# Second attention: weight products in halves over two steps, weight splits at places of their own, the last square summed alone

## The reference, cut to what matters

```python
qg = rms_norm_2(x, norm_g) @ w_in              # 1024 -> 2048: queries and gates
q, gate = qg[..., :DIFF_WIDTH], qg[..., DIFF_WIDTH:]
scores = einsum("qd,kd->qk", q_hi, k_hi) / 8 - slope[h] * |qpos - kpos|     # for h in 8 heads, i in 2
probs = softmax(where(allowed, scores, -inf))
weights = probs[:, :, 0] - lam * probs[:, :, 1]
out = einsum("qk,ke->qe", weights, v)          # per block of 128 queries and head
out = rms_norm_2(out, sub_g) * (1.0 - lambda_init)
x = x + (out * silu(gate)) @ w_out
return rms_norm_2(x, final_norm_g)             # the last norm of the whole model
```

## Time and profile before

| what | value |
|---|---|
| time, median of 3 runs | 2152.75 us (2152.07 to 2153.59) |
| the profiled execution | 2152.05 us, of it 2150.2 us from first to last instruction |
| PE busy | 2006.3 us (93%) |
| DVE busy | 1397.0 us (65%) |
| ACT busy | 856.6 us (40%) |
| mean granted TensorE clock | 0.974 of full |
| the loop of the second attention, 1918.8 to 2111.7 us | 192.90 us, PE busy 173.69, DVE 139.11, ACT 108.30 |

### The profile page before, as it was taken

How to read it: one execution, slowest core, us unless ns; L and a number is a source line. 1 busy time by engine, 2 the same in 40 slices (tenths; PEclk the granted TensorE clock), 3 DMA queues, 4 the chain that set the end, 5 groups by cost and what they waited for, 6 DMA issues and landing times.

```text
span 2150.2 us, 24817 instructions
## 1 busy us (share of the span) xinstructions
PE 2006.3 (93%) x9332; PEld 1574.0 (73%) x9332; DVE 1397.0 (65%) x2060; ACT 856.6 (40%) x1332; POOL 264.8 (12%) x241
## 2 busy tenths in 40 slices
PE   6789999999999999999999999989999989999887
PEld 4567878888887766778888886767777767876555
DVE  7895467536645458657636646877877786437875
ACT  4454333222233348633222234434343434236653
POOL 5130100000010000010000000333323232000002
PEclk9897999999999999999999999999999999999998
DMA  5364323233232220023232222212222213321002
GB/s 195 108 136 119 107 79 108 81 106 98 80 107 98 89 79 1 20 80 107 82 115 91 84 91 81 68 54 64 70 68 69 75 54 98 98 89 39 30 25 74
DMA packets 79479, 178.33 MB, mean 83 GB/s; under 512 B 17664, under 2 KB 31104, under 8 KB 79360
## 3 DMA queue, kind: packets, MB, share of 16 engines
q1 hardware_dynamic: 75648, 169.46, 25.5%
q0 software_dynamic: 3424, 6.23, 1.0%
q10 hardware_dynamic: 288, 1.05, 0.2%
HBM read 169.43 MB, written 7.27 MB: 82 GB/s over the span
## 4 chain that ended last, share of the span: by engine, by line
PE 64%; DVE 21%; ACT 8%; issue 6%; DMA 0%; POOL 0%; SPq 0%; DVEq 0%; POOLq 0%; ACTq 0%
PE psum L408 16%; PE psum L411 16%; PE psum L409 16%; DVE wl L379 3%; PE psum L428 2%; PE psum L431 2%; PE psum L429 2%; PE psum L778 1%; PE psum L779 1%; PE psum L780 1%; ACT wh L368 1%; DVE mbc L1443 1%; DVE mE L1567 1%; DVE mE L1586 1%; DVE mE L1587 1%
## 5 line engine op out<-in xcount | busy, mean ns | idle before, releaser
L379 DVE TENSOR_TENSOR wl<-raw,wh 128x1024 fp32r<-128x1024 f32 (+3 forms) x337 | 390.0, 1158 | 368.6 <-ACT wh L368 368.1
L408 PE MATMUL psum<-xh,wh 128*128 128x512 f32 x1480 | 592.5, 400 | 15.1 <-DVE h L604 10.9
L411 PE MATMUL psum<-xh,wl 128*128 128x512 f32 x1480 | 580.6, 392 | 1.9 <-DVE wl L379 1.9
L409 PE MATMUL psum<-xl,wh 128*128 128x512 f32 x1480 | 580.0, 392 | 0.0
L368 ACT ACTIVATE wh<-raw 128x1024 fp32r<-128x1024 f32 (+3 forms) x337 | 314.4, 937 | 289.3 <-PE psum L411 181.3
L408 PEld LDWEIGHTS psum<-xh,wh 128*128 128x128 f32 x1480 | 280.4, 189 | 91.2 <-issue 13.6
L411 PEld LDWEIGHTS psum<-xh,wl 128*128 128x128 f32 x1480 | 280.0, 189 | 63.9 <-DVE wl L379 4.5
L409 PEld LDWEIGHTS psum<-xl,wh 128*128 128x128 f32 x1480 | 280.1, 189 | 60.6 <-issue 3.7
L527 POOL TENSOR_TENSOR rs<-rs,sq 128x512 f32<-128x512 f32 x49 | 67.2, 1372 | 1127.1 <-ACT sq L512 1126.3
L408 PE MATMUL psum<-fh,wh 128*128 128x512 f32 x352 | 139.1, 395 | 0.0
L411 PE MATMUL psum<-fh,wl 128*128 128x512 f32 x352 | 139.1, 395 | 0.0
(11 more groups left out here) (446 smaller groups left out, 3127.0 us busy)
## 6 DMA issues: line engine op xcount, KB each, us to landing
raw<-d_w SPq DMA_DIRECT2D x224, 512.0 KB, 3.5
raw<-d_w SPq DMA_DIRECT2D x32, 384.0 KB, 3.0
raw<-d_w SPq DMA_DIRECT2D x48, 256.0 KB, 2.6
raw<-d_w SPq DMA_DIRECT2D x32, 320.0 KB, 2.9
Mt<-d_kd SPq DMA_DIRECT2D x64, 64.0 KB, 2.4
bc<-d_bc SPq DMA_DIRECT2D x8, 256.0 KB, 4.1
d_ud<-ust SPq DMA_DIRECT2D x8, 256.0 KB, 2.4
U<-d_ud POOLq DMA_DIRECT2D x64, 32.0 KB, 2.4
```

What stands on the lines that cost most here:

```text
L379: dve.e.tensor_tensor(K.wl[n % NH][:, 0:COLS[n]], K.raw[n % RAW][:, 0:COLS[n]], K.wh[n % NH][:, 0:COLS[n]].bitcast(F32), ALU.subtract).the ...
L408: pe.e.matmul(b[:, :], WH[:, o:o + P], XH, start=(k == k0), stop=False)
L409: pe.e.matmul(b[:, :], WH[:, o:o + P], XL, start=False, stop=False)
L411: mm = pe.e.matmul(b[:, :], WL[:, o:o + P], XH, start=False, stop=(k == k1 - 1))
```

## The change

Four edits, all in the second attention and the last norm. (1) Each of the 14 products in the loop is cut into two halves of 12 matmuls: the first half stays in the product's step n, the second stands in step n + 1, into the same bank. What reads the product (`queryB`, `gateB`, `gateT`, `gateC`) comes one step later. (2) ACT's high split (`queryH`, `gateH`) stands at the end of step n - 1, behind `keep`, and DVE's low split (`queryL`, `gateL`) in step n behind `combine`, ahead of `keep`. (3) `sumsq` moves from the last entries of a step to the first of the next one. (4) In the last norm POOL adds six squares to the first instead of seven, and PE adds the eighth by a second matmul with the matrix of ones into the same bank.

```diff
     dense = [x for m in range(8) for x in ([("query", m + 2)] if m < 6 else []) + [("gate", m)]]
-    at = {(k * 31 + 6) // 13: x for k, x in enumerate(dense)}
-    assert len(at) == 14 and max(at) < 33
+    first = {(k * 31 + 6) // 13: x for k, x in enumerate(dense)}
+    second = {n + 1: x for n, x in first.items()}
+    assert len(first) == 14 and max(second) < 33 and not set(first) & set(second)
     out = [("query", 0), ("queryB", 0), ("query", 1), ("queryB", 1)]
+    out.append((first[0][0] + "H", first[0][1]))
...
-        if n in at:
-            what, m = at[n]
-            out.append((what, m))
+        if n in first:
+            out.append(first[n])
+        if n in second:
+            what, m = second[n]
+            out.append((what + "2", m))
             later.setdefault((n + 1, "first"), []).append((what + "B", m))
...
             out.append(("combine", n - 2))
+        if n in first:
+            out.append((first[n][0] + "L", first[n][1]))
         if 0 <= n - 3 < 32:
             out.append(("keep", n - 3))
+        if n + 1 in first:
+            out.append((first[n + 1][0] + "H", first[n + 1][1]))
+        if 0 <= n - 3 < 32:
             if (n - 3) % 4 == 3:
                 hd = (n - 3) // 4
-                for k, what in enumerate(("mix", "sumsq", "rs", "tailA", "tailB", "split")):
-                    later.setdefault((n + 1 + k, "last"), []).append((what, hd))
+                for k, what in ((1, "mix"), (3, "rs"), (4, "tailA"), (5, "tailB"), (6, "split")):
+                    later.setdefault((n + k, "last"), []).append((what, hd))
                 later.setdefault((n + 2, "first"), []).append(("square", hd))
+                later.setdefault((n + 3, "first"), []).append(("sumsq", hd))
...
+def product_half(K, pe, name, m, bank, x, freed, half):
+
+    if half == 0:
+        take(pe, bank, freed)
+        pe.begun = next_unit(K, pe, name, "T", m, 0)
+    n, WH, WL = pe.begun
+    b = K.bank[bank]
+    pe.wait_ge("hi", n + 1)
+    for k in range(4 * half, 4 * half + 4):
+        o = k * P
+        XH, XL = x(k)
+        pe.e.matmul(b[:, :], WH[:, o:o + P], XH, start=(k == 0), stop=False)
+        pe.e.matmul(b[:, :], WH[:, o:o + P], XL, start=False, stop=False)
+        pe.wait_ge("lo", n + 1)
+        mm = pe.e.matmul(b[:, :], WL[:, o:o + P], XH, start=False, stop=(k == 7))
+    if half:
+        mm.then_inc(K.S["unit"], 1)
...
-    for k in range(1, 8):
+    for k in range(1, 7 if b == 6 else 8):
...
-    pe.wait_ge("acc", 7 * (b + 1))
+    pe.wait_ge("acc", 7 * b + 6 if b == 6 else 7 * (b + 1))
...
-    pe.e.matmul(K.bank[bank][:, :], K.con("ones"), K.acc[:, :], start=True, stop=True).then_inc(K.S["ssum"], 1)
+    mm = pe.e.matmul(K.bank[bank][:, :], K.con("ones"), K.acc[:, :], start=True, stop=(b != 6))
+    if b == 6:
+        pe.wait_ge("sq", 8 * b + 8)
+        mm = pe.e.matmul(K.bank[bank][:, :], K.con("ones"), K.sq[1][:, :], start=False, stop=True)
+    mm.then_inc(K.S["ssum"], 1)
```

More of the change, by code:

```diff
@@ L2582, in att2_pe @@
     for what, m in ATT2_ORDER:
[L2583 to L2586, removed]
+        if what in ("query", "query2") and m > 1:
+            product_half(K, pe, "b_w_in_2", m, B2[("query", m)], x, ("aqc", m + 1), int(what == "query2"))
+        elif what in ("gate", "gate2"):
+            product_half(K, pe, "b_w_in_2", 8 + m, B2[("gate", m)], x, ("agg", m + 1), int(what == "gate2"))
         elif what == "out":
@@ L2612, in att2_act @@
     for what, m in ATT2_ORDER:
-        if what in ("query", "gate", "out"):
-            split_hi(K, act, done(*tile2(what, m)) + LA)
+        if what in ("queryH", "gateH", "out") or (what == "query" and m < 2):
+            split_hi(K, act, done(*tile2(what.strip("H"), m)) + LA)
         elif what == "gateT":
@@ L2653, in att2_dve @@
     for what, m in ATT2_ORDER:
-        if what in ("query", "gate", "out"):
-            split_lo(K, dve, done(*tile2(what, m)) + LA)
+        if what in ("queryL", "gateL", "out") or (what == "query" and m < 2):
+            split_lo(K, dve, done(*tile2(what.strip("L"), m)) + LA)
         elif what == "queryB":
```

## The result

The changed kernel takes 2127.84 us (median of 4 runs, 2126.09 to 2129.58) against 2153.17 us in the same comparison: ratio 0.9879, interval 0.9862 to 0.9896, 22 to 30 us less. The forecast was 2138.0 us and a range of 2131 to 2147. The profiled execution took 2129.55 us, 22.5 less than the one before.

What follows compares the result with a forecast made beforehand. PE was taken as the bound, idle 19.2 us in the second attention's loop through hand-over order. Terms -13.2 + 2.5 - 2.5 + 0 - 1.2 = -14.4 us gave 2138.0 us against the middle of two times, range 2131 to 2147.

Steps and rivals of the forecast that it cites:

- Idle time: Second attention's loop: PE's 19.2 us of waits fall to 6, saving 13.2 us.
- Busy time: PE's 173.69 us in the loop, given no net change: 2.5 us more for hand-overs, 2.5 less for clock.
- Hand-overs: PE in the loop: entering and leaving 14 more product groups costs 2.5 us, bounds 0 to 2.8.
- Clock: Two loop stretches behind idle time: the granted clock should stay up, saving 2.5 us, bounds 0 to 3.2.
- Table loads: ACT gets four more, 12 become 16, at 1.28 us each; costed at 0, or 5.1 us if all show.
- The last square: Last norm's end: PE sums the eighth square by its own matmul, saving 1.0 to 1.3 us, 1.2 taken.
- nearly all idle time goes: Rival for the loop: 1 us of PE idle time left, hand-overs at 0, about 2130 us; chance 0.10.
- Nothing comes of it, the waits change places: Rival for the loop: PE keeps 17 us of idle time and pays 2.5 us, giving 2151.5 us; chance 0.06.
- the pacemaker: Rival: DVE paces the loop, idle 12 us instead of 6, about 2145.5 us; chance 0.15.
- one sign of being wrong: In the loop, DVE showing up as releaser of `scores` in steps that hold a half; no size given.
- the other signs: Changed profile: `sumsq` waits in only two heads, DVE's high-split wait near zero, `turn` waiting for `keep` at most 6.2 us.
- ACT's double switches: Rival: `rs` and tanh with loads, 4.5 us, delay `keep` in steps 9, 10, 34, 35; about 2159 us, chance 0.03.

Runs made afterwards that it cites:

- splits only: Kernel before with only the high and low splits moved to places of their own, whole products in their old steps: 2137.1 us, ratio 0.9927.
- halves only: Kernel before with only the products cut into halves, both splits left in the first half's entry ahead of `exps`: 2154.8 us, ratio 1.0009.
- the pair experiment: Kernel before with PE waiting for both banks of a step's two score products ahead of the first: 2153.6 us, ratio 0.9992.

## Why the prediction was right or wrong

In the profiled executions 22.5 us went where 14.4 were forecast. Nearly all of the difference is PE's busy time, which the sum left as it was and which fell by 8.0 us. A second step failed without moving the sum: the idle time was put down to the wrong edit.

**Idle time: right in size, wrong in its cause.** Of 19.2 us I forecast 13.2 to go; 13.7 went. But the forecast wrote them to the halves, wait by wait, and counted "nothing for it by itself" for the splits. The experiments say the opposite: splits only leaves 9.5 us of idle time, halves only 19.3. The step that failed is the sentence that DVE's waiting "counts only where PE waits" followed by a list in which each of PE's waits was removed by a half. The second paragraph of the prediction had it right: three of the four waits have one origin, DVE sitting behind the high split. The halves need that origin gone; then they remove part of the rest. That the size fits is partly luck. Of the 6 us that I left, wait by wait, `sumsq` had 1.6 and took 3.1, `turn` 1.5 and took none, `scores` 1.5 and took 0.5, the output product 0.4 and took 1.0, and `mix`, for which I had none, took 0.8. For `sumsq` in heads 2 and 5 the forecast was 0.8 each and 0.65 came; the wait of 1.81 in head 4 is new with the change.

**Busy time: the missing term, 8.0 us.** The sum took PE's 173.69 busy us for work and let them stand; this is the step that put the time below the range. Counted from the start of each record to the next one's, less idle time, the two loops divide as follows. The score pairs take 29.5 us before and 24.4 after (5.1 less), `turn` 12.5 and 10.8 (1.7 less), the output products 25.2 and 23.6 (1.6 less), `sumsq` 8.0 and 6.9 (1.2 less), `mix` the same within 0.1, and the query and gate products 80.5 and 82.1 (1.6 more, the hand-overs). Of the score pairs' 5.1 us, 4.1 are hidden waiting: the late starts of the second products, 4.7 us before and 0.6 after, whose nature the pair experiment shows. The clock runs across all groups with 3.6 us; most of what the output products and `sumsq` lost lies in rows at half clock (2090.9 to 2093.9, and the `sumsq` at 2059.08 with 2.05 us instead of 1.10). What shortened `turn` was not tested apart.

**Hand-overs: right, a little high.** A half followed by `turn` takes 2.86 to 2.88 us from its start to the next start, 12 times 0.228 and 0.12 to 0.15. For 14 more groups that is 1.7 to 2.1 us; forecast 2.5.

**Clock: right direction, undersized.** 2.5 forecast, 3.6 between these two executions. The order of the kernel before had 13.7, 20.3 and 23.4 us at half clock in three profiled executions, one of them with the pair waits. I took one execution's clock as the kernel's. The medians differ by 25.3 us and the profiles by 22.5, because the profiled execution of before lay 1.1 us below its median and that of the changed kernel 1.7 us above. The mean granted clock goes with this: the changed kernel's four runs are 2129.55 and 2129.58 us at 0.974, and 2126.09 and 2126.12 at 0.978 and 0.977. Over all 39 runs of the kernel before beside the experiments, from 2149.2 to 2161.3 us, 0.001 of mean clock goes with some 1 us. In the comparison with the changed kernel run again, the medians of the mean clock are 0.972 and 0.977; an estimate of the clock's share of the gain from these is some 5 us, twice the forecast. That the clock is the cause and not only goes along was not tested.

**Table loads: right.** 0 forecast; taking the four away moved no measured time and 2.2 us of idle time at most. The drain that the Trainium skill adds to a load ("ScalarE: Activation LUTs", "What ACT_TABLE_LOAD costs") does not show after the change either: the tanh starts 1.30 us after the load at 2022.53 began. Ahead of head 4's square a load does stand in PE's way, but together with a tanh and a high split, and moving the tanh took only 0.5 us off that wait.

**The last square: right.** 1.0 to 1.3 forecast, 1.31 in the trace, below what the time alone can tell.

**The rivals and the signs.** The number came out beside "nearly all idle time goes" (about 2130), but not by that mechanism: 5.5 us of idle time are left, not 1. "Nothing comes of it, the waits change places" is just what the halves do without the splits. DVE did not become the pacemaker: it is busy 82% of the loop. But one sign of being wrong did come, if only once and with 0.5 us: DVE released `scores` in step 5, which holds a half, and the same pair has the one hidden wait that is left:

```profile
1937.10 1.31 PE L2463 MATMUL psum<-k2T,q2T 64*128 64x256 f32 x4 [0.47 <-DVE small L2475]
```

Of the other signs, `sumsq` waits in three heads and not in two, and DVE's wait for the high split is 6.7 us and not near zero. ACT's double switches cost nothing that makes a sign.

## What to carry to other kernels

On an engine with a strict list, look at what its wait is queued in front of, and move the producer first: taking a copy of 1.05 us, once per product, out of the step in which another engine needs it was worth 16 us, while filling up the idle steps of the bound engine was worth nothing until then and some 10 us afterwards, part of it clock. Test two edits apart and together: here they brought 16 and 0 us apart and 26 together. And the busy share of a profile is here an upper bound of the work: operations that can run side by side but are released one after the other hide their wait in it.

## What the runs showed of the hardware that was not expected

The granted clock of identical instruction lists fell at different places in different executions (0.73 against 1.00 in the same 6 us, above). Behind gaps of PE of 1.01 and 2.01 us it fell in one execution and stayed up in the other, so here the program alone did not fix it.

Score products of 64 rows each, on the two halves of the rows, overlap when released together: they start 6 or 7 ns apart, and a pair of 64x128 takes 0.49 us against 0.96 staggered.

A DVE operation on one element per partition, 0.16 us elsewhere, took 1.20 us in the kernel before while POOL's subtraction ran, in two places of the loop. Timeline of both engines at the first:

```profile
1979.36 1.27 POOL L2556 TENSOR_TENSOR ol<-q2T,oh 128x512 fp32r<-128x512 f32 x1 [159.16 <-ACT oh L2550]
...
1979.45 1.20 DVE L2463 TENSOR_TENSOR small<-small,lam 128x1 f32<-128x1 f32 x1
```

Both end at 1980.6. After the change other DVE lines meet POOL: the second operation of `combine` takes 1.66 and 1.67 us in the two places where it begins under POOL's subtraction, and at most 0.75 elsewhere, so its mean is 608 ns where it had 552. Why the two engines hold each other up was not tested.
